# RWKV chunk products as 64x64 blocks on quarters of the TensorE array, without the padded operand and the block-diagonal tiles

## The reference, cut to what matters

```python
def step(S, inp):
    wt, kkt, kat, kt, vt, rt = inp
    S = (S * wt[..., None, :]
         - jnp.einsum('...vk,...k->...v', S, kkt)[..., :, None] * kat[..., None, :]
         + vt[..., :, None] * kt[..., None, :])
    return S, jnp.einsum('...vk,...k->...v', S, rt)
_, y = lax.scan(step, S0, xs)      # 2 directions x 4 heads, 1024 steps
```

## Time and profile before

| | |
|---|---|
| median of 3 runs | 2155.39 us (2149.98 to 2155.61) |
| profiled execution, first to last instruction (span) | 2151.9 us, 3.5 us under the median |
| rounds, forward direction | 630.7 to 831 us of the span |
| rounds, backward direction | 870.6 to 1073 us of the span |
| one round in the middle | 49 us, PE busy for nearly all of it |
| granted TensorE clock, mean of the span | 0.958 of full speed |

### The profile page before, as it was taken

How to read it: one execution, slowest core, us unless ns; L and a number is a source line. 1 busy time by engine, 2 the same in 40 slices (tenths; PEclk the granted TensorE clock), 3 DMA queues, 4 the chain that set the end, 5 groups by cost and what they waited for, 6 DMA issues and landing times.

```text
span 2151.9 us, 31739 instructions
## 1 busy us (share of the span) xinstructions
PE 1965.1 (91%) x13425; PEld 1711.6 (80%) x13425; DVE 829.1 (39%) x1339; ACT 663.1 (31%) x1288; POOL 638.5 (30%) x534
## 2 busy tenths in 40 slices
PE   5997887998779995799999898899999999999997
PEld 4896776787558884688889877778889988899887
DVE  4006887142554456545441414412122221222215
ACT  4215776213562223222131524422121111111112
POOL 3214552220263333433352510113122221222220
PEclk9999999999789998899999999899999999999999
DMA  5110000210000000000032210111111111111112
...
DMA packets 67725, 81.40 MB, mean 38 GB/s; under 512 B 4594, under 2 KB 62992, under 8 KB 67584
## 3 DMA queue, kind: packets, MB, share of 16 engines
...
q0 software_dynamic: 960, 2.78, 0.5%
...
## 4 chain that ended last, share of the span: by engine, by line
PE 80%; DVE 11%; ACT 4%; issue 1%; DMA 1%; POOL 1%; DVEq 0%; ACTq 0%; SPq 0%
PE PS L1662 17%; PE PS L1425 12%; PE PS L1426 11%; PE PS L1428 11%; PE PS L1438 7%; PE PS L1440 7%; PE PS L1439 7%; PE PS L1520 2%; DVE E__69 L1008 1%; PE PS L1554 1%; PE PS L1546 1%; DVE E__69 L1036 1%; DVE XN L934 1%; DMA XT<-in_x 1%; ACT CP L866 1%
## 5 line engine op out<-in xcount | busy, mean ns | idle before, releaser
L403 POOL TENSOR_TENSOR WL<-RAW,WH 128x512 fp32r<-128x512 f32 x228 | 309.0, 1363 | 980.5 <-ACT WH L540 980.4
L1425 PE MATMUL PS<-HH,WH 128*128 128x512 f32 x1072 | 422.0, 394 | 11.4 <-POOL WL L403 8.9
L1426 PE MATMUL PS<-HL,WH 128*128 128x512 f32 x1072 | 420.7, 392 | 0.0
L540 ACT ACTIVATE WH<-RAW 128x512 fp32r<-128x512 f32 x228 | 141.5, 631 | 694.1 <-PE PS L1428 333.1
L1428 PE MATMUL PS<-HH,WL 128*128 128x512 f32 x1072 | 332.9, 392 | 0.0
L1425 PEld LDWEIGHTS PS<-HH,WH 128*128 128x128 f32 x1072 | 203.7, 190 | 54.5 <-issue 8.3
L1438 PE MATMUL PS<-WH,AH 128*128 128x256 f32 x864 | 244.9, 284 | 1.4 <-DVE AL L1346 1.4
L1439 PE MATMUL PS<-WL,AH 128*128 128x256 f32 x864 | 244.5, 283 | 0.0
L1440 PE MATMUL PS<-WH,AL 128*128 128x256 f32 x864 | 244.5, 283 | 0.0
L1426 PEld LDWEIGHTS PS<-HL,WH 128*128 128x128 f32 x1072 | 203.7, 190 | 42.0
L1428 PEld LDWEIGHTS PS<-HH,WL 128*128 128x128 f32 x1072 | 203.0, 189 | 42.7
...
## 6 DMA issues: line engine op xcount, KB each, us to landing
...
```

Of the source, the lines that this page charges most:

```text
L403: pool.tensor_tensor(WL[:, p % NW], RAW[:, p % NRAW], WH[:, p % NW].bitcast(F32), ALU.subtract).then_inc(w_lo, 1)
L540: act.activation(WH[:, p % NW], RAW[:, p % NRAW], ACT.Copy).then_inc(w_hi, 1)
L1425: pe.matmul(where(ct, i), wh[:, k, c], ah(kt)[:, t0:t0 + n], start=first and starts(ct, i), stop=False, skip_group_check=True)
L1426: pe.matmul(where(ct, i), wh[:, k, c], al(kt)[:, t0:t0 + n], start=False, stop=False, skip_group_check=True)
```

## The change

- Every product of the stage becomes a 64x64 (or 64x64 by 128 columns) product of one chunk and one head. Operand rows 0 to 63 or 64 to 127 and result partitions 0 to 63 or 64 to 127 choose one of four quarters of the array. The tuple `QUADS` orders them so that neighbours in the order differ in rows, columns or both.
- `PAD`, `BT`, `KT`, the `pad` copies on ACT, the clearing on POOL and the semaphores `pad_zero` and `pad_done` go. Operands are read straight from `KR` and `BKt`.
- `G`, `QQ`, `LT`, `XX` hold the 64x64 blocks alone, so the elementwise operations on DVE, ACT and POOL in the levels and the head have half the elements. `G` gets a third column block for the transposed keys, filled by one ACT copy of 512 elements.
- All six transposes of a slot come first; the transposed products of a slot come right after its other products, and wait for ACT's copy.
- At the close, 24 + 12 products per slot become 40: eight with 128 columns, 32 with 64. DVE's six operations per slot become four.
- In the backward direction ACT waits for `r_ks` before its first copy (`G` of slot 1 lies where `KDN` was).

The diff, cut to its core (16 leading blanks taken off where lines are deep):

```diff
-self.G = at(n + "G", b, [2, 4, 2, P])
-self.PAD = at(n + "PAD", b + 8, [2, 2, 2, P])
-self.QQ = at(n + "QQ", b + 12, [2, 4, P])
-self.RH = at(n + "RH", b + 16, [4, 2, C])
-self.LT = at(n + "LT", b + 18, [4, P])
-self.XX = at(n + "XX", b + 20, [4, P])
-self.WU = at(n + "WU", b + 22, [4, 2, C])
-self.BT = at(n + "BT", 132 + 2 * i, [4, C])
-self.KT = at(n + "KT", 133 + 2 * i, [4, C])
+self.G = at(n + "G", b, [2, 4, 3, C])
+self.QQ = at(n + "QQ", b + 6, [2, 4, C])
+self.RH = at(n + "RH", b + 8, [4, 2, C])
+self.LT = at(n + "LT", b + 10, [4, C])
+self.XX = at(n + "XX", b + 11, [4, C])
+self.WU = at(n + "WU", b + 12, [4, 2, C])
...
-        G_PE, G_ACT, G_DVE, G_POOL = 8 + 2 * LV + 2, 3 + LV + 1, 5 + LV + 1, 1 + LV
+        G_PE, G_ACT, G_DVE, G_POOL = 4 + 2 * LV + 2, 2 + LV + 1, 2 + LV + 1, 1 + LV
...
+        QUADS = ((0, 0), (1, 1), (0, 1), (1, 0))
...
-pool.memset(slots[1].PAD[:, :, :, :, :], 0.0)
-pool.wait_ge(r_exp, 7 * (d + 1))
-pool.memset(slots[0].PAD[:, :, :, :, :], 0.0).then_inc(pad_zero, 1)
...
-        pool.wait_ge(g_dve[i], G_DVE * n + 2)
-        qt = sl.QQ[:, 1]
-        link(pool.tensor_tensor(qt.rearrange("p u (c k) -> p u c k", c=2), sl.G[:, 0, :, 0, :].rearrange("p u (c k) -> p u c k", c=2),
-                                CN[:, lvl:lvl + 64].unsqueeze(1).unsqueeze(1).broadcast_to([P, 4, 2, C]), ALU.mult))
-        pool.tensor_tensor(qt, qt, ID.unsqueeze(1).broadcast_to([P, 4, P]), ALU.subtract).then_inc(g_pool[i], 1)
-        pool.tensor_tensor(sl.LT[:, :, :].rearrange("p u (c k) -> p u c k", c=2), sl.G[:, 0, :, 0, :].rearrange("p u (c k) -> p u c k", c=2),
-                           CN[:, lvl + 64:lvl + 128].unsqueeze(1).unsqueeze(1).broadcast_to([P, 4, 2, C]), ALU.mult).then_inc(g_pool[i], 1)
+        pool.wait_ge(g_dve[i], G_DVE * n + 1)
+        qt, at_ = sl.QQ[:, 1], sl.G[:, 0, :, 0, :]
+        link(pool.tensor_tensor(qt, at_, CN[:, lvl:lvl + 64].unsqueeze(1).broadcast_to([P, 4, C]), ALU.mult))
+        pool.tensor_tensor(qt, qt, I64.unsqueeze(1).broadcast_to([P, 4, C]), ALU.subtract).then_inc(g_pool[i], 1)
+        pool.tensor_tensor(sl.LT[:, :, :], at_, CN[:, lvl + 64:lvl + 128].unsqueeze(1).broadcast_to([P, 4, C]), ALU.mult).then_inc(g_pool[i], 1)
...
-def pad(i, m):
-
-    sl, t = slots[i], tile_of(d, m, i)
-    for hp in range(2):
-        rows = slice(64 * hp, 64 * hp + 64)
-        for kr in range(2):
-            a = act.activation(sl.PAD[rows, :, hp, kr, :].rearrange("p a (c k) -> p a c k", c=2), KR[rows, kr, :, 2 * t:2 * t + 2, :], ACT.Copy)
-    a.then_inc(pad_done[i], 1)
-
-act.wait_ge(r_pre, d + 1)
-act.wait_ge(pad_zero, d + 1)
-for i in range(2):
-    pad(i, 0)
+if d:
+    act.wait_ge(r_ks, 1)
...
-        act.activation(sl.RH[:, :, 0, :], PS[:, sl.bank + 3, 0:256].rearrange("p (u k) -> p u k", k=C), ACT.Copy)
-        act.activation(sl.BT[:, :, :], PS[:, sl.bank + 3, 256:512].rearrange("p (u k) -> p u k", k=C), ACT.Copy).then_inc(g_act[i], 1)
+        act.activation(sl.RH[:, :, 0, :], PS[:, sl.bank + 2, 0:256].rearrange("p (u k) -> p u k", k=C), ACT.Copy)
+        act.activation(sl.G[:, :, :, 2, :], PS[:, sl.bank + 2:sl.bank + 4, :].rearrange("p b (a u k) -> p b a u k", a=2, u=4)[:, :, 1], ACT.Copy).then_inc(g_act[i], 1)
     for i, sl in enumerate(slots):
-        act.wait_ge(g_pe[i], pe0 + 7)
-        act.activation(sl.KT[:, :, :], PS[:, sl.bank + 1, 0:256].rearrange("p (u k) -> p u k", k=C), ACT.Copy).then_inc(g_act[i], 1)
...
+        act.wait_ge(g_pe[i], pe0 + 4)
+        act.activation(sl.RH[:, :, 1, :], PS[:, sl.bank, 0:256].rearrange("p (u k) -> p u k", k=C), ACT.Copy).then_inc(g_act[i], 1)
     for l in range(LV):
         for i, sl in enumerate(slots):
-            act.activation(sl.XX[:, :, :].rearrange("p u k -> p (u k)"), PS[:, sl.bank + 3, :], ACT.Copy).then_inc(g_act[i], 1)
-        if l == 2 and m + 1 < NPR:
-            for i in range(2):
-                pad(i, m + 1)
+            act.activation(sl.XX[:, :, :].rearrange("p u k -> p (u k)"), PS[:, sl.bank + 3, 0:256], ACT.Copy).then_inc(g_act[i], 1)
...
-        for k in range(4):
-            dve.wait_ge(g_pe[i], pe0 + 2 + k)
-            kind, ct = k // 2, k % 2
-            TT(sl.G[:, kind, 2 * ct:2 * ct + 2].rearrange("p u r t -> p u (r t)"), PS[:, sl.bank + k, :].rearrange("p (u c) -> p u c", u=2),
-               MK[:, d, 0:256].unsqueeze(1).broadcast_to([P, 2, 256]), ALU.mult).then_inc(g_dve[i], 1)
-    for i, sl in enumerate(slots):
-        dve.wait_ge(g_pe[i], pe0 + 6)
+        dve.wait_ge(g_pe[i], pe0 + 2)
+        for hp in range(2):
+            ins = TT(sl.G[:, :, hp:4:2, 0:2, :].rearrange("p a u r t -> p a u (r t)"),
+                     PS[:, sl.bank + hp, :].rearrange("p (a u c) -> p a u c", a=2, u=2),
+                     MK[:, d, 0:2 * C].unsqueeze(1).unsqueeze(1).broadcast_to([P, 2, 2, 2 * C]), ALU.mult)
+        ins.then_inc(g_dve[i], 1)
+        dve.wait_ge(g_pe[i], pe0 + 3)
         q = sl.QQ[:, 0]
-        link(TT(q, PS[:, sl.bank, :].rearrange("p (u c) -> p u c", u=4), MK[:, d, 256:384].unsqueeze(1).broadcast_to([P, 4, P]), ALU.mult))
-        TT(q, q, ID.unsqueeze(1).broadcast_to([P, 4, P]), ALU.subtract).then_inc(g_dve[i], 1)
+        link(TT(q.rearrange("p (a h) c -> p a h c", a=2), PS[:, sl.bank + 2:sl.bank + 4, 0:2 * C].rearrange("p h (a c) -> p a h c", a=2),
+                MK[:, d, 2 * C:3 * C].unsqueeze(1).unsqueeze(1).broadcast_to([P, 2, 2, C]), ALU.mult))
+        TT(q, q, I64.unsqueeze(1).broadcast_to([P, 4, C]), ALU.subtract).then_inc(g_dve[i], 1)
...
+                qq = sl.QQ[:, :, :, :].rearrange("p a u k -> p (a u k)")
+                TT(qq, PS[:, sl.bank + 1, :], qq, ALU.add).then_inc(g_dve[i], 1)
...
+        TT(g, rm[:, :, :, 0, :], g, ALU.add)
+        TT(BKt[:, 0, :, pair, :], rm[:, :, :, 1, :], I64.unsqueeze(1).unsqueeze(1).broadcast_to([P, 2, 2, C]), ALU.add)
+        TT(BKt[:, 1, :, pair, :], nh[:, 0], DD.rearrange("p (a c) -> p a c", a=2)[:, :, pair].unsqueeze(3).broadcast_to([P, 2, 2, C]), ALU.mult)
...
-            pe.transpose(PS[:, b0 + 3, P * ct:P * ct + P], both(t, KR, 0, ct), ID)
-            mm = pe.transpose(PS[:, b0 + 3, 256 + P * ct:256 + P * ct + P], both(t, BKt, 0, ct), ID)
+            pe.transpose(PS[:, b0 + 2, P * ct:P * ct + P], both(t, KR, 0, ct), ID)
+            for kind in range(2):
+                mm = pe.transpose(PS[:, b0 + 2 + kind, 256 + P * ct:256 + P * ct + P], both(t, BKt, kind, ct), ID)
         mm.then_inc(g_pe[i], 1)
-        pe.wait_ge(pad_done[i], n + 1)
-        for k in range(4):
-            if k == 3:
-                pe.wait_ge(g_act[i], ac0 + 1)
-            kind, ct = k // 2, k % 2
-            mm1(PS[:, b0 + k, :], both(t, BKt, kind, ct), sl.PAD[:, ct].rearrange("p u r t -> p (u r t)")).then_inc(g_pe[i], 1)
+        for kind in range(2):
+            for ct in range(2):
+                for hp, c in QUADS:
+                    r = slice(64 * hp, 64 * hp + 64)
+                    f = 256 * kind + 128 * ct
+                    mm = mm1(PS[64 * c:64 * c + 64, b0 + hp, f:f + 128], BKt[r, kind, ct, 2 * t + c, :], KR[r, :, ct, 2 * t + c, :])
+        mm.then_inc(g_pe[i], 1)
+        pe.wait_ge(g_act[i], ac0 + 1)
+        for ct in range(2):
+            for hp, c in QUADS:
+                r = slice(64 * hp, 64 * hp + 64)
+                mm = mm1(PS[64 * c:64 * c + 64, b0 + 2 + hp, 64 * ct:64 * ct + 64], KR[r, 0, ct, 2 * t + c, :], BKt[r, 0, ct, 2 * t + c, :])
+        mm.then_inc(g_pe[i], 1)
     for i, sl in enumerate(slots):
         t, b0 = tile_of(d, m, i), sl.bank
         pe.wait_ge(g_dve[i], dv0 + 1)
         for u in range(4):
-            mm = mm1(PS[:, b0, P * u:P * u + P], sl.PAD[:, u // 2, u % 2, 0, :], both(t, BKt, 0, u // 2))
-        mm.then_inc(g_pe[i], 1)
-        pe.wait_ge(g_dve[i], dv0 + 2)
-        for ct in range(2):
-            mm = pe.transpose(PS[:, b0 + 1, P * ct:P * ct + P], both(t, BKt, 1, ct), ID)
-        mm.then_inc(g_pe[i], 1)
-        pe.wait_ge(g_dve[i], dv0 + 4)
...
+            for c in range(2):
+                r = slice(64 * c, 64 * c + 64)
+                mm = mm1(PS[r, b0, 64 * u:64 * u + 64], sl.G[r, 1, u, 0, :], VT[r, t, 64 * u:64 * u + 64])
...
-                mm = mm1(PS[:, sl.bank + 3, P * u:P * u + P], sl.LT[:, u, :], sl.QQ[:, 0, u, :])
+                for c in range(2):
+                    r = slice(64 * c, 64 * c + 64)
+                    mm = mm1(PS[r, sl.bank + 3, 64 * u:64 * u + 64], sl.LT[r, u, :], sl.QQ[r, 0, u, :])
...
-                    mm1(PS[:, sl.bank, P * u:P * u + P], sl.QQ[:, 1, u, :], sl.XX[:, u, :])
+                    for c in range(2):
+                        r = slice(64 * c, 64 * c + 64)
+                        mm1(PS[r, sl.bank + 1, 64 * u:64 * u + 64], sl.QQ[r, 1, u, :], sl.XX[r, u, :])
             for u in range(4):
-                mm = mm1(PS[:, sl.bank + 1, P * u:P * u + P], sl.XX[:, u, :], sl.QQ[:, 1, u, :])
+                for c in range(2):
+                    r = slice(64 * c, 64 * c + 64)
```

(76 more changed lines are left out.)

27 lines of the change are left out of this document (11 added, 16 removed).

## The result

The changed kernel takes **1999.62 us** (median of 4 runs, 1994.96 to 2000.44). The kernel before took 2155.5 us beside it (4 runs, 2149.98 to 2155.97). The ratio is **0.928, with a 95% interval of 0.9265 to 0.930**: 156 us less, where 130 were forecast. The time lies in the predicted range (1995 to 2055), 5 us above its low end.

The account below looks back on a forecast made before the run. PE, busy 91% of the span, was taken as the bound. Rounds of 33.0 us against 48.9 save 15.9 in six, 16.3 in two; with small parts 2151.9 - 130 = 2022, plus 3.5: 2025 us, range 1995 to 2055.

Parts of the forecast that it names:

- head, to slot 1's first product: Round's start: transposes, first products, DVE's masks, then POOL's `QQ` and `LT`, a new wait; 9.7 us, before 11.5.
- three levels: Chain of 80 PE records at 29 ns and DVE's 0.69 us addition by turns; 3.32 us each, before 6.1.
- the fourth: Level in which `state_out` adds 32 records, so PE's own work exceeds the chain; 3.95 us.
- last level to closing: Slot 1's first product, `RH` products of both slots and slot 0's `WU`, up to the first closing block; 3.7 us.
- closing: Round's end: per slot 16 records at 55 ns and 64 at 29, two slots and a switch; 5.7 us.
- So I take 29 ns, for both patterns: Price of a 64x64 record on PE, on the diagonal pair or on all four quarters: 29 ns.
- I take 55: Price of a 64x64 product's record with 128 columns, absent from the trace: 55 ns, with 29 as the lower end.
- this case: Rival: four quarters work at once at N=64 too, records at 14 ns in head and closing; 1990 us, chance 0.08.
- POOL at 0.66: Price of a POOL mask of 256 elements in the head: 0.66 us, between 0.64 and 0.90.
- The clock's rivals: Clock drops for part of each round (2045 to 2053 us, chance 0.2) or stays low (2180 to 2235, chance 0.05).
- Quarters taking turns on one bank: Rival: quarters writing one PSUM bank take turns, doubling `VT`,`G`, level and `RH` records; 2135 us, chance 0.04.
- Hidden work: `pad` copies on ACT, smaller DVE closing operations and dropped `BT`, `KT` copies: cost nothing before, covered by PE's queue.

Follow-up runs that it names:

- e3: The kernel before, with only its 24 closing 64x64 products of a slot turned over the four quarters: 2139.65 us, ratio 0.9947 to the kernel before.
- e4: The changed kernel with POOL making `LT` before `QQ` for each slot in the head: 1985.29 us, ratio 0.9231 to the kernel before.
- e7: The changed kernel with a level's second products made by pairs of heads and DVE's addition in two halves: 1991.48 us, ratio 0.9259 to the kernel before.
- e5: The changed kernel with level results written to two banks, still on the diagonal quarters (a control): 1999.35 us, ratio 0.9293 to the kernel before.
- e6: The changed kernel with level products on all four quarters and two banks, part of the output not the reference's: 1982.15 us, ratio 0.9211 to the kernel before.
- e2: The changed kernel with closing products one quarter at a time, all five steps in a row: 2037.92 us, ratio 0.947 to the kernel before.
- e1: The changed kernel with closing products done for the diagonal pair of quarters, then for the other pair: 2006.48 us, ratio 0.9333 to the kernel before.

## Why the prediction was right, and where its sizes were off

The mechanism was as told in the main: PE's work in a round falls from 48.9 to 26.5 us, the chain in the levels keeps its form, and POOL becomes the new wait in the head. The sum was 27 us too high, and that it still met the range was in part luck, as told below. By its terms, in the round that starts at 850.16:

| part | forecast | measured |
|---|---|---|
| head, to slot 1's first product | 9.7 | 8.09 |
| three levels | 3.32 each | 3.51, 3.42, 3.42 |
| the fourth | 3.95 | 3.99 |
| last level to closing | 3.7 | 3.67 |
| closing | 5.7 | 3.19 |
| sum | 33.0 | 29.29 |

- **The mis-sized term is the price of a record on four quarters.** "So I take 29 ns, for both patterns" and "I take 55" for 128 columns took the rate of two quarters for that of four. With 14.5 and 27 ns the closing needs some 2.8 us less (2.5 were measured, as the new wait for DVE is in it) and the head some 1.8 less (0.9 for each slot's N=128 products). `e3` showed on the kernel before that the earlier trace rows was read wrongly: that the products touched four quarters didn't mean that four worked at once. I gave this case 0.08, with 1990 us for it, outside my range; it held in the head and the closing, and 1990 is nearer to the median of 1999.6 than 2025 is. The evidence against it ("four quarters are no faster than two") was of an order, not of the array.
- **Luck.** By that rival's own sum a round is 33.0 less 2.5 and 1.9, 28.6 us, and measured rounds take 29.3 to 31.0. The range was met by 5 us because terms that I had too low or left out (the levels, DVE at the end of a round, "issue" gaps) gave back a part of what four quarters gained. The first rounds went the other way: I took their slow start to cost the same before and after, and they save 20.5 and 20.4 us instead of 16.3.
- **POOL at 0.66** was slightly low: 0.72, 0.79 and 0.72 by the groups, 2.28 for the three instead of 2.13. With the earlier start the head ends at 8.09. I had its path through DVE's masks of slot 1; by the chain it is POOL's own queue, slot 0's three operations and then slot 1's, with DVE done 0.08 us sooner. `e4` bears on this queue.
- **The levels at 3.32** (their terms add up to 3.30) were 0.1 low: 2.56 for the 80 records against 2.51, and the hand-over from DVE to PE is 0.14, not 0.05. That PE's own work lies below the chain was right, but not by as much as 3.01 says: in `e7`, with PE alone as the chain, a level takes 3.27 (857.42 to 860.69) instead of 3.42.
- **The clock's rivals** (0.25 together) didn't come: 1.00 in all six rounds that are not the first of their direction (0.90 and 0.92 in those), with PE idle for 1.26 us and its weight loads for 1.40 in the head (the row at 858.25). In `e5` and `e6` it did dip, as told above.
- **Quarters taking turns on one bank** (0.04): a level's products in both row halves write one bank, and records of the two start 6 ns apart (861.756, 861.762), 29 ns a record on two quarters with 58 on one (`e2`). `e1`'s pairs, which write two banks, start 6 ns apart and run at 29 ns too. So no wait of one for the other shows. The rule of the Trainium skill, TensorEngine Tiling (Array Packing), Restrictions and Gotchas, on row tiles and one bank, doesn't hold for this pattern.
- **The floor.** The Trainium skill, TensorE: Matmul & The Clock Gate, in the part on the 56 ns, would have no start-to-start time below about 25 ns. The traces disagree: 14.5 ns in two kernels, at a clock of 1.00.
- **Hidden work** stayed hidden with one exception, which I had put at nothing: at the end of a round DVE's closing operations end last, and PE waits 0.26 us for them (the row at 879.49). Two rounds that are not the first of their direction take 30.45 and 29.81 us instead of 29.3. They have 0.89 and 0.55 us near the end of their closing blocks that the chain calls "issue" (at 718.03 and 849.41). It was not forecast; the last section tells what the traces say of it.
- **Around the span** I added 3.5 us, and the profiled execution had 1.8; the median lies 4.7 above it, within the spread of the runs.
